# A mixture-of-experts decoder layer on one core: the order in which the groups of experts are visited

## What is computed

```python
pg_top, grp = lax.top_k(pg, 1)
pe_top, e_local = lax.top_k(jax.nn.softmax(le, axis=-1), TOP_K_INNER)
gate = pg_top * pe_top / jnp.sum(pe_top, axis=-1, keepdims=True)
expert = grp * EXPERTS_PER_GROUP + e_local
...
def block_fn(args):
    tok, wt, e = args
    xb = x2[tok]
    hb = jax.nn.silu(xb @ w_gate[e]) * (xb @ w_up[e])
    return (hb @ w_down[e]) * wt[:, None].astype(xb.dtype)
```

## Time and profile before

| | |
|---|---|
| median of three runs | 1514.29 us (1513.65 to 1516.33) |
| the profiled execution | 1511.85 us, its span 1509.9 us |
| TensorE matmuls, busy | 1270.7 us (84%), 6908 records |
| VectorE / ScalarE / GpSimd busy | 334.1 / 232.3 / 12.7 us |
| mean granted TensorE clock | 0.941 |
| moved by DMA | 480.29 MB, mean 318 GB/s |

### The profile page before, as it was taken

How to read it: one execution, slowest core, us unless ns; L and a number is a source line. 1 busy time by engine, 2 the same in 40 slices (tenths; PEclk the granted TensorE clock), 3 DMA queues, 4 the chain that set the end, 5 groups by cost and what they waited for, 6 DMA issues and landing times.

```text
span 1509.9 us, 16581 instructions
## 1 busy us (share of the span) xinstructions
PE 1270.7 (84%) x6908; PEld 650.4 (43%) x6908; DVE 334.1 (22%) x748; ACT 232.3 (15%) x532; POOL 12.7 (1%) x78
## 2 busy tenths in 40 slices
PE   7999999999999998858779988778686876858565
PEld 6889876766544453313233424232231323213111
DVE  2096510173731041110111120111111011110103
ACT  2001120144610111101010111010010101101002
POOL 1000000000001000000000000000000000000000
PEclk9999999999999999989999999989898998988978
DMA  9845563334437299999999799999999999999995
GB/s 304 234 159 170 165 214 122 113 73 94 115 136 223 112 365 356 393 420 422 420 421 419 295 422 421 421 421 421 421 420 422 421 421 421 421 421 421 421 422 239
DMA packets 132700, 480.29 MB, mean 318 GB/s; under 512 B 16429, under 2 KB 82193, under 8 KB 82705
## 3 DMA queue, kind: packets, MB, share of 16 engines
q1 hardware_dynamic: 126256, 477.59, 81.4%
q10 hardware_dynamic: 6368, 1.63, 0.6%
HBM read 477.09 MB, written 2.10 MB: 317 GB/s over the span
## 4 chain that ended last, share of the span: by engine, by line
PE 52%; DMA 26%; SPq 17%; DVE 2%; issue 1%; ACT 1%; ACTq 0%; DVEq 0%
DMA ring<-in_expert_w_up_dram 17%; SPq L568 17%; PE PS L890 13%; PE PS L987 7%; PE PS L1122 5%; PE PS L1155 4%; DMA ring<-in_expert_w_down_dram 4%; PE PS L879 4%; DMA spare<-in_expert_w_down_dram 3%; PE PS L910 3%; PE PS L1182 3%; PE PS L1113 2%; DMA spare<-in_expert_w_up_dram 2%; PE PS L1133 2%; PE PS L1166 2%
## 5 line engine op out<-in xcount | busy, mean ns | idle before, releaser
L1133 PE MATMUL PS<-ring,XG 128*32 128x512 f32 x1216 | 197.4, 786 | 133.9 <-DMA ring<-in_expert_w_up_dram 133.9
L890 PE MATMUL PS<-hT,ring 128*128 128x256 f32 x768 | 166.6, 379 | 0.0
L1133 PEld LDWEIGHTS PS<-ring,XG 128*32 128x32 f32 x1216 | 38.4, 127 | 279.3 <-DMA ring<-in_expert_w_up_dram 202.9
L890 PEld LDWEIGHTS PS<-hT,ring 128*128 128x128 f32 x768 | 145.8, 190 | 20.1 <-issue 0.5
L1122 PE MATMUL PS<-ring,XG 128*64 128x512 f32 x592 | 132.8, 596 | 17.4 <-DMA ring<-in_expert_w_up_dram 17.0
L987 PE MATMUL PS<-ring,mix 128*128 128x512 f32 x256 | 111.4, 594 | 0.4 <-ACT mix L1484 0.4
L2197 DVE TENSOR_TENSOR hTe<-PS,sg 128x128 f32<-128x128 f32 (+1 forms) x33 | 11.0, 333 | 430.3 <-ACT sg L1675 430.2
L1668 ACT ACTIVATE Hs<-PS 128x512 f32<-128x512 f32 x33 | 19.7, 597 | 518.0 <-PE PS L1133 361.2
L1182 PE MATMUL PS<-Y,SW 128*128 128x512 f32 x176 | 93.6, 638 | 0.5 <-ACT Y L1687 0.5
L1166 PE MATMUL PS<-ring,hTe 128*32 128x512 f32 x592 | 72.7, 620 | 24.3 <-DMA ring<-in_expert_w_down_dram 24.1
L2083 DVE TENSOR_TENSOR x<-PS,x 128x1024 f32<-128x1024 f32 x44 | 53.9, 1224 | 159.5 <-PE PS L1182 159.5
(11 more groups left out here) (356 smaller groups left out, 956.6 us busy)
## 6 DMA issues: line engine op xcount, KB each, us to landing
ring<-in_expert_w_gate_dram SPq DMA_DIRECT2D x109, 1024.0 KB, 26.3
ring<-in_expert_w_up_dram SPq DMA_DIRECT2D x109, 1024.0 KB, 27.5
ring<-in_expert_w_down_dram SPq DMA_DIRECT2D x53, 2048.0 KB, 29.1
ring<-in_w_in_dram SPq DMA_DIRECT2D x22, 2048.0 KB, 9.6
spare<-in_expert_w_down_dram SPq DMA_DIRECT2D x10, 2048.0 KB, 28.8
spare<-in_expert_w_gate_dram SPq DMA_DIRECT2D x18, 1024.0 KB, 26.7
spare<-in_expert_w_up_dram SPq DMA_DIRECT2D x18, 1024.0 KB, 27.5
ring<-in_w_out_dram SPq DMA_DIRECT2D x32, 256.0 KB, 7.8
```

Of the source, the lines that this page charges most:

```text
L890: mm = pe.matmul(dst, lhs, rhs, start=(k == 0), stop=(k == DK - 1))
L1133: mm = pe.matmul(PS[r:r + 32, 0, :], XG[:, part, 4 * c + j, column:column + 32], w[u][:, j, :], start=(c == 0 and pair == 0), stop=(c == 3 ...
```

## The change

One line gives another order of the same eleven groups. The small group in second place goes to the end, where two small groups now stand; four mixed groups stand between the fixed group and the twin where there was one small and one mixed; three mixed groups stand behind the twin where there were six. The twin's load is number 14, counted from 0, and was number 9.

```diff
-GROUP_ORDER = ["fixed", "small", "mixed", "twin", "mixed", "mixed", "mixed", "mixed", "mixed", "mixed", "small"]
+GROUP_ORDER = ["fixed", "mixed", "mixed", "mixed", "mixed", "twin", "mixed", "mixed", "mixed", "small", "small"]
```

## The result

The changed kernel takes 1520.87 us (median of six runs, 1519.53 to 1522.5); the kernel before took 1514.78 us in six runs, three of them those above (1513.65 to 1517.36). The ratio is 1.0035 with a 95% interval of 1.0023 to 1.0047, so the change costs 3.5 to 7.1 us: 5.3 by the ratio, 6.1 by the two medians. The forecast was +1.7 us, and 1520.87 lies above the range (1520.0). The profiled execution took 1520.23 us with a span of 1518.2, 8.3 us more than the one before.

What follows compares the result with a forecast made beforehand. Expert weight loading at about 421 GB/s was taken as the bound, so only empty-queue time could change. Terms 0 + 1.7 + 0 + 0 = +1.7 us on the median 1514.29 gave 1516.0 us, range 1512.8 to 1520.0.

Steps and rivals of the forecast that it cites:

- The first wide expert: Behind the fixed group, group 1's first chunk is wide and released later while the queue is dry: +1.7 us.
- Rival B: TensorE stays behind through the first wide expert, releasing more slots late: between 1.7 and 11.6, say +6 us, 1520.3; chance 0.07.
- The twin moves from load 9 to load 14 ... 0 us: At the twin, the stall takes the same 11.4 us wherever it stands, if TensorE has caught up before: 0 us.
- Cost 0, by count: Whole program: same visits, gathers, scatter pieces, and chunks to the same slots in the same order: 0 us.
- Two small groups at the end ... 0 us, at the clock of these rows: Tail: only work after the last landing counts, and the last four visits are narrow in both orders: 0 us.
- rival A: Tail at half clock: down half and scatters double, +9.0 us, 1525.0; only the down half, +1.9; chance 0.05.

Runs made afterwards that it cites:

- the exchanged groups: Kernel before with only its second and third group exchanged (fixed, mixed, small, twin, six mixed, small), twin still at load 9: 1519.36 us, 1.0020.
- the small group behind the late twin: Changed kernel with one small group taken from the end and put directly behind the twin: 1517.19 us, 1.0012 to the kernel before.
- more instructions: Changed kernel with 80 unused one-column matmuls in each of 12 narrow visits behind the twin: 1521.05 us, 1.0037 to the kernel before.
- the small group behind the early twin: Kernel before with its last small group put directly behind the twin: 1513.94 us, 0.9993.
- both kernels with fillers: Unused matmuls, two ahead of the twin's second down product, two ahead of the last down half: changed kernel 1518.61 us, kernel before 1516.22 us.
- the changed order with scatters in the wait: Changed kernel with two scatters moved into TensorE's wait ahead of the twin's second down product: 1517.80 us, 1.0011 to the kernel before.
- the second set: Changed kernel run once more with no edit: 1521.64 us, 1.0039 to the kernel before.

## Why the prediction was wrong

**The first wide expert, +1.7 us: right,** in place, mechanism and size, in each of the profiles of an order with a mixed group second. The row behind the twin that it was read from gave 3.82 us, and 3.82 came. Rival B (TensorE stays behind through the expert) did not happen: 421 GB/s from 620 to 962.

**"The twin moves from load 9 to load 14 ... 0 us": wrong as the sum needed it.** Its dry spells are TensorE's chain and nothing else, as argued, and that chain did not depend on where the twin stands. But its length was taken at the clock of one profile. Of the nine profiles in which the wait for DVE stands unfilled, TensorE came back from it at half clock in six (both of the changed kernel, the exchanged groups, the late twin, the small group behind the late twin, more instructions) and at full clock in three: both of the kernel before and the small group behind the early twin, whose order up to the twin is that of before. The half clock costs 1.7 us: from the last gate chunk to SP's first issue behind the gather it is 54.8 us in all five at half clock with a wide expert behind the twin, and 53.1 in both profiles of before and in both kernels with fillers. The runs in which the wait is filled, with idle matmuls or with scatters, show that the clock is what costs it. The length of the wait does not decide it, as 2.18 us went with either level and 1.91 us too, nor does the twin's place, as the exchanged order falls with its twin at load 9. What decides it is left open; no run separated it. The late twin alone, moved to load 15, paid it in its profile and showed no cost in its times, so how often the order pays it is known only for the changed kernel, where filling the two waits took 2 to 3 us off the time.

**"Cost 0, by count" for the work, and the stream at 421 GB/s with no history: the term that was missing.** The number of TensorE's instructions is the same; how many of their blocks fall into one unbroken stretch of loading is not. Before, the stretches held 7 and 22 blocks, and two jumps showed; with the twin in the middle they hold 13 and 17, and three did, the third in the last two landings. +1.3 us. That a dry spell lets the 16 engines start together again, and so starts the count anew, would give this. The 1.1 us lost unevenly ahead of the twin's hole fit it, the late twin's jump at the 3rd block does not. The size of a jump is measured; that it is this term which the times of the changed kernel pay is argued, from two profiles that agree. The Trainium skill has the fetch itself in "Runtime: NRT & Kernel Launch", section "Instruction fetch mechanics": blocks of 16 KiB on a queue of their own, the cost of a boundary "mostly hidden". The trace agrees with the size: 56 packets bring 0.92 MB. For TensorE the cost stays small here ("issue" is 1% of the chain that ended last), for the full stream it does not: one engine is taken for 1.1 us each time, and about every eighth time the landings move by some 1.2 to 1.6.

**"Two small groups at the end ... 0 us, at the clock of these rows": wrong by 1.5.** The down half ran at half clock in both profiles of the changed kernel and in the changed order with scatters in the wait, and at full clock with a mixed group ahead of the last small one. That is the lesser case of rival A, which was named there at +1.9 and given no chance apart from the worse case of 9.0; the scatters stayed at full clock (7.11 us). The rule that I weighed, of the Trainium skill's page "TensorE: Matmul & The Clock Gate", section "HAM oscillation — how this bites in real kernels", puts a short burst of matmuls behind a wait for DMA at half rate. The trace agrees at this place in these three profiles (3.57, 3.37 and 3.33 us for 1.92). It is not a matter of the late landing alone: in the run with more instructions TensorE waited 2.89 us there, longer than the 2.52 here, and kept the full clock.

So 1.7 + 1.7 + 1.3 + 1.5 = 6.2 us, against 5.3 by the ratio of the first six runs, 5.9 by that of the second set, and by the medians 6.1 and, for the second set, 5.6. The agreement is not proof of each term, since the half clock at the twin and the added jump come from profiles that also show them for the late twin alone, whose times show nothing. The forecast had the first of four terms. The other three were all listed as zero on the ground that the order does not change the work, and the only one priced as a rival was held to be unlikely. The range shows the same: its top took in half of rival B and left no room for several small costs of the same sign.

## What to carry to other kernels

Where loading is the bound, read what follows each dry spell: the first piece of work behind it should release its buffer soonest, so the narrow expert belongs there; a wide one there cost 1.7 us behind the fixed group, and a narrow one saved 1.6 to 1.7 behind the twin. A wait of TensorE on a chain that holds buffers is best filled with needed work, since it costs its own length and possibly a slower clock behind it. A profile of one execution fixes neither the clock behind such a wait nor its price; take both levels into the sum.

## What the runs showed of the hardware

Landings in a full stream of loads jump in step with the fetching of TensorE's instructions. Each block of 16 KB took an engine for about 1.1 us, and behind the twin the landings of 2 MB chunks moved by some 1.2 to 1.6 us at every eighth block, with 17 blocks in 470 us as with 31. That blocks go to eight engines in turn would give this; only the counts are shown, and why the first jump came at the 9th block in most stretches and at the 3rd in one is open. Matmuls added in waiting time are thus not quite free: the 960 small ones (12 visits of 80) came with one jump more and 1.0 to 1.4 us in the profile, though not in the time.

The time of this program also varies ahead of anything changed here: the gather for group 1 began between 600.8 and 605.2 us in thirteen profiles. The granted clock from 14 to 20 us goes with it: 1.00 in the three that began by 601.4, 0.72 to 0.75 in the seven from 602.0 to 603.1, and 0.50 to 0.55 in the three from 604.3 on.
